# Post-norm of a sublayer's outputs: inverse root formed per token as a column and spread by TensorE, with one weight cast moved ahead of it on ScalarE

## The chip, the cores and the metric

The kernel runs on one NeuronCore of a Trainium2 chip. The metric is the device time of one execution in microseconds (us), as the median of several executions. Lower is better.

## The reference, cut to what matters

Two layers, each of three sublayers: a feed-forward block, a mixer of two head groups, a second feed-forward block. Each sublayer has an RMS norm before it and one behind it:

```python
def rms_norm(x, g=None):
    y = xf * lax.rsqrt(jnp.mean(jnp.square(xf), axis=-1, keepdims=True) + EPS)
...
def gated_post(x, o, g, mods, j, coef):
    return x + coef * mods[:, 3 * j + 2, None] * rms_norm(o, g)
...
    h = modulated_pre(x, norm_pre[l, 0], mods, 0)
    x = gated_post(x, swiglu(h, ffn_w1[l, 0], ffn_w3[l, 0], ffn_w2[l, 0]), norm_post[l, 0], mods, 0, 0.5)
```

There are 512 prompt frames and 32 sample frames, so 544 tokens in all, and D_MODEL is 1024. The change concerns `rms_norm(o, g)` inside `gated_post`: one number for each token, 1/sqrt(mean of squares + eps), by which all 1024 outputs of that token are multiplied. It happens six times in the program.

## The kernel before, in words

Activations lie transposed: features on the 128 partitions, tokens along the free dimension, so `x` is 8 tiles of 128 x 544. Sums over features are therefore sums over partitions, and TensorE makes them with a matmul.

Weights come from memory in chunks, into the two slots of `raw`. ACT (ScalarE) casts a chunk to `w_hi` (`high`, L936 to L947), POOL (GpSimd) forms the rest `w_lo` (`low`, L446), and PE (TensorE) multiplies with both. SP (SyncE) issues the load of a chunk when the low part of the chunk two before it is made (L343 to L344). Every engine has its own hand-written instruction stream; semaphores join them, and within a stream the order is that of the code.

The outputs of a sublayer come as 8 tiles (`out_tiles` on PE and on ACT), alternating between PSUM banks 0 and 1 and banks 2 and 3. For each, ACT squares the tile into `wide_s` (L1026) and evicts it to `o_buf` (`o_ffn` or `o_mix`), scaled by the gate (L1030, L1032). POOL adds the squares of tiles 0 to 6 into `squares` (L453, L457).

After the last output tile comes what is called the turn-over here:

- PE sums over partitions with a full matrix of ones, first `squares` (L633), then the last tile's squares (L635), both through `add_squares` (L543). Banks 4 and 5 then hold, on every one of the 128 partitions, the same 544 sums.
- ACT takes the square root of all 128 x 544 (`root_of`, L950).
- DVE (VectorE) takes the reciprocal of 128 x 544 (L1290) into banks 4 and 5, and then, for each of 8 tiles, forms the product with it (L1297). It adds the even tiles and the last to `x` (L1301), POOL the other odd ones (`add_odd`, L472).
- ACT starts the next sublayer with `pre_scale`: two small casts (L958), the cast of the next sublayer's second chunk (L960; the first was cast during the last output tile), then `h_hi` from each tile of `x` as it comes (L965), and squares of `x` (L975).
- POOL makes `w_lo` of the next sublayer's first two chunks (L477) ahead of its own additions to `x`.
- PE starts with `first_tiles` (L556 to L566) when `h_hi` of tile 0 and the two chunks are ready. DVE makes `h_lo` (L1316).

After the last sublayer there is no next one, and `x` is written out.

## Time and profile before

| | |
|---|---|
| median of 3 executions | 2578.21 us |
| lowest and highest | 2574.72 and 2578.86 us |
| the profiled execution, its own time | 2575.32 us |
| its span, first to last instruction | 2573.5 us |
| PE busy | 2374.8 us (92%) |
| DVE, POOL, ACT busy | 1318.2, 893.4, 812.6 us |
| granted TensorE clock, mean | 0.977 of full |

The profiled execution is one execution, and its time is that of the device, some 1.8 us above its span. A busy share is an average over the whole program; what sets the end is read from the chain of work that ended last, and at a given place from the idle time in front of an instruction and the name of what ended it.

### The profile page before, as it was taken

How to read it: one execution, taken by the hardware profiler on the slowest of the kernel's cores; microseconds unless marked ns; L12 is line 12 of the kernel's file. 1: busy time of each engine (PE TensorE's matmuls, PEld its weight loads, DVE VectorE, ACT ScalarE, POOL GpSimd, SP SyncE). 2: the span in 40 equal slices, each digit the busy share in tenths (PEclk: the TensorE clock that was granted, in tenths of full speed). 3: DMA queues.
4: the chain of work that ended last, by engine and by line, in shares of the span. 5: the costliest groups of instructions: out<-in, count | busy, mean ns of one | idle time of the engine just before them, and what ended most of it. 6: DMA issues, size and time to landing. Idle time of an engine off the chain costs nothing.

```text
span 2573.5 us, 43848 instructions
## 1 busy us (share of the span) xinstructions
PE 2374.8 (92%) x17486; PEld 2231.6 (87%) x17486; DVE 1318.2 (51%) x2006; ACT 812.6 (32%) x1371; POOL 893.4 (35%) x384
## 2 busy tenths in 40 slices
PE   1999999899788899999989999989988898999996
PEld 1999999899456899999989999989964588999996
DVE  7333379784473333337253335986835515333552
ACT  2322322433223433223243223234323334223321
POOL 1333334443000544344444343444420034333342
PEclk9999999999899999999999999999989999999998
DMA  6222268323100122226312224761220011222551
GB/s 222 76 88 84 90 236 280 116 88 112 33 1 6 61 89 83 89 89 248 122 57 82 90 81 155 281 221 66 82 71 33 1 50 59 89 84 87 182 197 57
DMA packets 71507, 272.48 MB, mean 106 GB/s; under 512 B 8640, under 2 KB 10048, under 8 KB 70528
## 3 DMA queue, kind: packets, MB, share of 16 engines
q1 hardware_dynamic: 71424, 271.35, 30.6%
q8 instruction: 55, 0.90, 0.1%
q14 instruction: 28, 0.23, 0.0%
HBM read 267.87 MB, written 3.45 MB: 105 GB/s over the span
## 4 chain that ended last, share of the span: by engine, by line
PE 75%; DVE 12%; issue 6%; ACT 3%; DMA 1%; POOL 1%; DVEq 0%; SPq 0%; POOLq 0%; ACTq 0%
PE ps L534 21%; PE ps L533 21%; PE ps L537 21%; PE ps L543 2%; PE ps L831 2%; PE ps L875 2%; DVE ret_q L1407 1%; PE ps L827 1%; DVE ret_k L1407 1%; DVE wide_v L1297 1%; DVE x L1301 1%; PE ps L566 1%; DVE wide_v L1256 1%; POOL w_lo L446 1%; DVE ps L1290 1%
## 5 line engine op out<-in xcount | busy, mean ns | idle before, releaser
L446 POOL TENSOR_TENSOR w_lo<-raw,w_hi 128x1024 fp32r<-128x1024 f32 (+1 forms) x304 | 790.7, 2601 | 1609.8 <-ACT w_hi L947 1294.1
L533 PE MATMUL ps<-h_hi,w_hi 128*128 128x274 f32 x3296 | 897.0, 290 | 5.3 <-DVE z_tmp L1376 5.3
L534 PE MATMUL ps<-h_lo,w_hi 128*128 128x274 f32 x3296 | 900.7, 290 | 0.0
L537 PE MATMUL ps<-h_hi,w_lo 128*128 128x274 f32 x3296 | 686.7, 289 | 0.0
L533 PEld LDWEIGHTS ps<-h_hi,w_hi 128*128 128x128 f32 x3296 | 624.9, 190 | 6.8 <-issue 6.7
L534 PEld LDWEIGHTS ps<-h_lo,w_hi 128*128 128x128 f32 x3296 | 621.7, 189 | 0.2
L947 ACT CAST w_hi<-raw 128x1024 fp32r<-128x1024 f32 (+1 forms) x236 | 268.7, 1138 | 877.3 <-PE ps L537 689.8
L537 PEld LDWEIGHTS ps<-h_hi,w_lo 128*128 128x128 f32 x3296 | 522.0, 188 | 0.0
L533 PE MATMUL ps<-u_hi,w_hi 128*128 128x272 f32 x1408 | 382.4, 289 | 12.9 <-POOL w_lo L446 12.9
L534 PE MATMUL ps<-u_lo,w_hi 128*128 128x272 f32 x1408 | 380.8, 289 | 0.0
L1256 DVE CUSTOM_DVE_ANT_0 wide_v<-ada_w,ps 128x1024 bf16<-128x1024 f32 x288 | 332.1, 1217 | 46.5 <-DMA ada_w<-in_ada 29.3
L1334 DVE TENSOR_TENSOR wide_v<-ps,wide_rinv 128x548 f32<-128x548 f32 x88 | 64.1, 729 | 449.3 <-PE ps L537 449.3
L537 PE MATMUL ps<-u_hi,w_lo 128*128 128x272 f32 x1408 | 292.5, 289 | 0.0
L533 PEld LDWEIGHTS ps<-u_hi,w_hi 128*128 128x128 f32 x1408 | 266.0, 189 | 14.6 <-POOL w_lo L446 14.5
L534 PEld LDWEIGHTS ps<-u_lo,w_hi 128*128 128x128 f32 x1408 | 265.6, 189 | 0.0
L1339 DVE SCALAR_TENSOR_TENSOR wide_v<-wide_v,wide_s 128x512 f32<-128x512 f32 (+1 forms) x176 | 194.2, 1142 | 110.2 <-ACT wide_s L998 110.2
L537 PEld LDWEIGHTS ps<-u_hi,w_lo 128*128 128x128 f32 x1408 | 220.5, 188 | 0.0
L556 PE MATMUL ps<-h_hi,w_hi 128*128 128x274 f32 x192 | 63.0, 350 | 91.7 <-ACT h_hi L965 69.9
L1290 DVE RECIPROCAL ps<-root 128x544 f32<-128x544 f32 x6 | 21.4, 3560 | 217.6 <-ACT root L950 217.6
L556 PEld LDWEIGHTS ps<-h_hi,w_hi 128*128 128x128 f32 x192 | 44.3, 231 | 98.2 <-issue 74.1
L1001 ACT CAST u_hi<-wide_v 128x544 f32 (+1 forms) x88 | 57.0, 648 | 214.1 <-DVE wide_v L1339 214.1
L940 ACT CAST w_hi<-raw 128x1024 fp32r<-128x1024 f32 x68 | 71.1, 1046 | 167.1 <-PE ps L537 102.1
(219 smaller groups left out, 2552.5 us busy)
## 6 DMA issues: line engine op xcount, KB each, us to landing
raw<-in_w_up SPq DMA_DIRECT2D x176, 512.0 KB, 3.3
ada_w<-in_ada SPq DMA_DIRECT2D x160, 512.0 KB, 4.4
raw<-in_w_dn SPq DMA_DIRECT2D x64, 704.0 KB, 4.7
raw<-in_w_mix SPq DMA_DIRECT2D x64, 512.0 KB, 3.3
decay<-in_decay SPq DMA_DIRECT2D x2, 2048.0 KB, 8.3
x<-in_x SPq DMA_DIRECT2D x1, 2176.0 KB, 9.1
rope_tab<-in_rope SPq DMA_DIRECT2D x2, 1088.0 KB, 4.9
out_y<-x SPq DMA_DIRECT2D x1, 2176.0 KB, 7.3
```

The costliest lines, as they stand in the source:

```text
L446: pool.tensor_tensor(w_lo[:, slot, 0:width], raw[:, slot, 0:width], w_hi[:, slot, 0:width].bitcast(F32), ALU.subtract).then_inc(lo_done.se ...
L533: pe.matmul(ps[:, bank + t, 0:half], wh, hi[:, n], start=start, stop=False)
L534: pe.matmul(ps[:, bank + t, 0:half], wh, lo[:, n], start=False, stop=False)
L537: last = pe.matmul(ps[:, bank + t, 0:half], wl, hi[:, n], start=False, stop=stop)
L543: last = pe.matmul(ps[:, bank + t, 0:HT], mat[:, :], src[:, t * HT:(t + 1) * HT], start=start, stop=stop)
L556: pe.matmul(ps[:, 2 * w + t, 0:HW], w_hi[:, w, k * P:(k + 1) * P], h_hi[:, k, n], start=k == 0, stop=False)
L940: nc.scalar.copy(w_hi[:, slot, 0:width], raw[:, slot, 0:width]).then_inc(hi_done.sem, 1)
L947: nc.scalar.copy(w_hi[:, k, 0:width], raw[:, k, 0:width]).then_inc(hi_done.sem, 1)
L1001: nc.scalar.copy(u_hi[:, bass.ds(i * 2 + f, 1), :].rearrange("p a n -> p (a n)"), tmp_v[:, f, :]).then_inc(up_hi.sem, 1)
L1256: v_.tensor_tensor_reduce(junk[v], ada_w[:, t, :], c_row, 1.0, 0.0, ALU.mult, ALU.add, acc[:, v, t:t + 1]).then_inc(ada_done.sem, 1)
L1334: v_.tensor_tensor(halves(wide_v[:, f, :]), wide_pair(4 * f + 2), halves(wide_rinv[:, :]), ALU.mult)\
L1339: v_.scalar_tensor_tensor(out=wide_v[:, f, at], in0=wide_v[:, f, at], scalar=wide_v[:, f, T + 2 * v:T + 2 * v + 1], in1=wide_s[:, f, at], ...
```

## The change

- PE: the sums are formed with the tokens on the partitions. For each of five blocks of 128 tokens (at 0, 128, 256, 384 and 416, the last one overlapping) the squares are the stationary operand and one column of ones is the moving one (`token_sums`). The result is 128 x 5 in a corner of bank 5.
- ACT: the root is of 128 x 5 (`token_root`). It stands between the last square and the last tile's evictions, no longer behind them.
- ACT: the cast of the next sublayer's second chunk stands between the last square and `token_root`, no longer in `pre_scale` (except for the first sublayer, which has nothing ahead of it).
- DVE: the reciprocal is of 128 x 5.
- PE: five transposes (`spread`) of those columns, each broadcast along the free dimension, put the 544 inverses on all 128 partitions of banks 4 and 5, now as 544 neighbouring columns.
- DVE: each product waits for its own tile's eviction, no longer for all eight ahead of the first.

```diff
+TOK_AT = [0, P, 2 * P, 3 * P, T - P]
+TOK = len(TOK_AT)
+SUM_AT = 2 * NS
...
+            def token_sums(src, bank, start, stop):
+
+                for b, at in enumerate(TOK_AT):
+                    last = pe.matmul(by_token(bank)[:, b:b + 1], src[:, at:at + P], ones[:, 0:1],
+                                     start=start and b == 0, stop=stop, skip_group_check=True)
+                return last
+
+            def spread(l, n, bank):
+
+                pe.wait_ge(inverted.sem, inverted.at(l, 2 * n + 2))
+                for b in range(4):
+                    pe.transpose(ps[:, bank, b * P:(b + 1) * P], tok_inv[:, b:b + 1].to_broadcast([P, P]), ident[:, :])
+                pe.transpose(ps[:, bank + 1, 0:NS], tok_inv[P - NS:P, 4:5].to_broadcast([NS, P]),
+                             ident[P - NS:P, P - NS:P]).then_inc(inv_spread.sem, 1)
...
-                add_squares(squares[:, :], 4, True, False, ones)
+                token_sums(squares[:, :], 4, True, False)
                 pe.wait_ge(out_sq.sem, out_sq.at(l, (j + 1) * KD))
-                add_squares(tmp_s[:, 1, :], 4, False, True, ones).then_inc(sums.sem, 1)
+                token_sums(tmp_s[:, 1, :], 4, False, True).then_inc(sums.sem, 1)
+                spread(l, j, 4)
...
+            def token_root(l, n, bank):
+                nc.scalar.activation(tok_root[:, :], by_token(bank), ACT.Sqrt, bias=eps[:, 0:1], scale=1.0 / D)\
+                    .then_inc(rooted.sem, 1)
...
-                high(l, next_chunk + 1, 1, KD * P)
+                if not (l or j):
+                    high(l, next_chunk + 1, 1, KD * P)
...
                     nc.scalar.activation(halves(tmp_s[:, mm, :]), pair(2 * mm), ACT.Square).then_inc(out_sq.sem, 1)
+                    if m == KD - 1:
+                        if next_chunk is not None:
+                            high(next_chunk[0], next_chunk[1] + 1, 1, KD * P)
+                        act.wait_ge(sums.sem, sums.at(l, (j + 1) * SUMS))
+                        token_root(l, 2 * j + 1, 4)
...
-                act.wait_ge(sums.sem, sums.at(l, (j + 1) * SUMS))
-                root_of(l, rooted, 2 * j + 1, 4, D)
...
-                    v_.reciprocal(out_inv, halves(root[:, :])).then_inc(inverted.sem, 1)
-                    dve.wait_ge(inverted.sem, inverted.at(l, 2 * j + 2))
-                    dve.wait_ge(out_ev.sem, out_ev.at(l, (j + 1) * KD))
+                    v_.reciprocal(tok_inv[:, :], tok_root[:, :]).then_inc(inverted.sem, 1)
+                    dve.wait_ge(inv_spread.sem, inv_spread.at(l, j + 1))
                     for m in range(KD):
+                        dve.wait_ge(out_ev.sem, out_ev.at(l, j * KD + m + 1))
...
-                        v_.tensor_tensor(halves(tmp_v[:, m % 2, :]), halves(o_buf[:, m, :]), out_inv, ALU.mult)\
+                        v_.tensor_tensor(tmp_v[:, m % 2, :], o_buf[:, m, :], along(4), ALU.mult)\
```

On ACT, at the last output tile of the first feed-forward block and the start of the mixer, these instructions stand in the stream before the change (`L940` casts a weight chunk, `L1026` squares, `L1030` and `L1032` evict, `L950` is the root, `L965` makes `h_hi`):

```order
L940 CAST w_hi<-raw 128x1024
L1026 ACTIVATE wide_s<-ps 128x544
L1030 ACTIVATE o_ffn<-ps,mul_post 128x272
L1030 ACTIVATE o_ffn<-ps,mul_post 128x240
L1032 ACTIVATE o_ffn<-ps,mul_post 128x32
L950 ACTIVATE root<-ps,eps 128x544
L958 CAST h_hi<-mods 128x8x2 x2
L940 CAST w_hi<-raw 128x1024
L965 ACTIVATE h_hi<-x,mul_pre 128x512
```

The same stretch of ACT's stream with the change (the line numbers are those of the changed kernel; `L968` casts, `L1059` squares, `L982` is `token_root`, `L998` makes `h_hi`):

```order
L968 CAST w_hi<-raw 128x1024
L1059 ACTIVATE wide_s<-ps 128x544
L968 CAST w_hi<-raw 128x1024
L982 ACTIVATE tok_root<-ps,eps 128x5
L1068 ACTIVATE o_ffn<-ps,mul_post 128x272
L1068 ACTIVATE o_ffn<-ps,mul_post 128x240
L1070 ACTIVATE o_ffn<-ps,mul_post 128x32
L990 CAST h_hi<-mods 128x8x2 x2
L998 ACTIVATE h_hi<-x,mul_pre 128x512
```

The second cast moved from behind the root to directly behind the square, and the root moved ahead of the three evictions.

On PE, between the last output tile and `first_tiles` of the mixer, this stands in the stream before (one row of this listing is a matmul of the program, which the trace shows as two passes where its operands are plain 32-bit floats):

```order
L537 MATMUL ps<-u_hi,w_lo 128x272 x2
L626 REGISTER_ALU
L626 COMPARE_AND_BRANCH
L543 MATMUL ps<-squares,ones 128x272 x2
L543 MATMUL ps<-wide_s,ones 128x272 x2
L556 MATMUL ps<-h_hi,w_hi 128x274
```

And this with the change:

```order
L549 MATMUL ps<-u_hi,w_lo 128x272 x2
L653 REGISTER_ALU
L653 COMPARE_AND_BRANCH
L562 MATMUL ps<-ones,squares 128x1 x5
L562 MATMUL ps<-ones,wide_s 128x1 x5
L570 MATMUL ps<-ident,tok_inv 128x128 x4
L571 MATMUL ps<-ident,tok_inv 128x32
L583 MATMUL ps<-h_hi,w_hi 128x274
```

Four wide matmuls became ten of one column, and five transposes, which wait for DVE, follow them ahead of the next sublayer's first matmul.

## Rows read from the trace of the kernel before

**Rows 1.** The page: the chain that ended last, shares of the span by engine.
```profile
PE 75%; DVE 12%; issue 6%; ACT 3%; DMA 1%; POOL 1%; DVEq 0%; SPq 0%; POOLq 0%; ACTq 0%
```

**Rows 2.** Instructions by line: the reciprocal (L1290) and the roots (L950); ns min/median/max.
```profile
L1290 DVE RECIPROCAL ps<-root x6: 3560/3560/3561, 473.8 to 2551.4; 128x544 f32<-128x544 f32 x6
...
L950 ACT ACTIVATE root<-ps,eps x16: 694/716/717, 73.1 to 2550.7; 128x544 f32<-128x544 f32 x16
```

**Rows 3.** Timeline of ACT, first turn-over: start us, us, what, [idle before <-releaser].
```profile
471.19 0.62 ACT L1026 ACTIVATE wide_s<-ps 128x544 f32<-128x544 f32 x1 [5.77 <-PE ps L537]
471.71 0.83 ACT L1030 ACTIVATE o_ffn<-ps,mul_post 128x272 f32<-128x272 f32 x2
...
473.09 0.72 ACT L950 ACTIVATE root<-ps,eps 128x544 f32<-128x544 f32 x1 [0.36 <-PE ps L543]
...
473.90 1.04 ACT L940 CAST w_hi<-raw 128x1024 fp32r<-128x1024 f32 x1
478.95 0.72 ACT L965 ACTIVATE h_hi<-x,mul_pre 128x512 fp32r<-128x512 f32 x1 [4.00 <-DVE x L1301]
```

**Rows 4.** Timeline of DVE, the same turn-over.
```profile
477.43 0.72 DVE L1297 TENSOR_TENSOR wide_v<-o_ffn,ps 128x544 f32<-128x544 f32 x1
478.19 0.72 DVE L1301 TENSOR_TENSOR x<-x,wide_v 128x544 f32<-128x544 f32 x1
478.83 1.34 DVE L1297 TENSOR_TENSOR wide_v<-o_ffn,ps 128x544 f32<-128x544 f32 x2
480.21 1.34 DVE L1301 TENSOR_TENSOR x<-x,wide_v 128x544 f32<-128x544 f32 x1
```

**Rows 5.** Timeline of POOL, the same turn-over.
```profile
475.02 2.34 POOL L446 TENSOR_TENSOR w_lo<-raw,w_hi 128x1024 fp32r<-128x1024 f32 x1 [7.13 <-ACT w_hi L940]
479.62 1.34 POOL L472 TENSOR_TENSOR x<-x,wide_v 128x544 f32<-128x544 f32 x1 [2.26 <-DVE wide_v L1297]
```

**Rows 6.** Timeline of PE and of its weight loads (PEld), the same turn-over.
```profile
470.99 1.08 PE L543 MATMUL ps<-squares,ones 128*128 128x272 f32 x4
471.90 1.14 PE L543 MATMUL ps<-wide_s,ones 128*128 128x272 f32 x4
...
471.86 0.76 PEld L543 LDWEIGHTS ps<-wide_s,ones 128*128 128x128 f32 x4 [0.23 <-ACT wide_s L1026]
```

**Rows 7.** Timelines of PE and PEld in the mixer: transposes, three weight loads, small matmuls.
```profile
640.97 1.91 PE L699 MATMUL ps<-ident,ret_v 128*128 128x128 f32 x16
...
708.25 0.30 PEld L831 LDWEIGHTS ps<-wide_s,q_pe 128*128 128x128 f32 x2
708.46 0.26 PEld L827 LDWEIGHTS ps<-kv,q_abs 128*128 128x128 f32 x1
...
652.17 0.42 PE L730 MATMUL ps<-ret_ss,v_tok 32*64 32x32 f32 x2
652.52 0.42 PE L731 MATMUL ps<-q_cross,state_in 128*64 128x32 f32 x2
```

**Rows 8.** Instructions by line, ns min/median/max: a small eviction, small reciprocal, the products.
```profile
L1032 ACT ACTIVATE o_ffn<-ps,mul_post x32: 288/296/299, 361.1 to 2550.0; 128x32 f32<-128x32 f32 x32
...
L1543 DVE RECIPROCAL inv_sum<-exp_sum x68: 152/153/165, 711.8 to 2066.8; 128x1 f32<-128x1 f32 x68
...
L1297 DVE TENSOR_TENSOR wide_v<-o_ffn,ps x32: 705/709/721, 477.4 to 2564.3; 128x544 f32<-128x544 f32 x32
```

**Rows 9.** Windows (busy PE PEld DVE ACT POOL, clock, DMA share, GB/s), first, last of four; SP timeline.
```profile
466.00:471.10 5.10, 5.10 (x43) 5.10 (x42) 2.37 (x10) 0.00 (x0) 1.89 (x1) 1.00 0.00 0
...
2123.00:2127.10 4.10, 4.10 (x34) 4.10 (x33) 0.00 (x0) 0.56 (x1) 2.56 (x2) 1.00 0.00 0
...
1283.72 18.47 SPq L344 DMA_DIRECT2D raw<-in_w_up  x3
```

**Rows 10.** Windows of PE alone (length, busy, granted clock, DMA share, GB/s), first turn-over.
```profile
473.10:479.90 6.80, 0.00 (x0) 0.74 0.81 303
479.90:483.00 3.10, 3.07 (x12) 0.50 0.08 30
```

More of the change, by code:

```diff
@@ L161, in streaming_trunk @@
         eps_root = sb("eps_root", [P, 1])
+        tok_root = sb("tok_root", [P, TOK])
+        tok_inv = sb("tok_inv", [P, TOK])
         neg_row = sb("neg_row", [P, 64])
@@ L223, in halves, with by_token, along @@
             return t.rearrange("p (t n) -> p t n", t=2)
-        out_inv = pair(4)
+        def by_token(bank):
+            return ps[:, bank + 1, SUM_AT:SUM_AT + TOK]
+        def along(bank):
+            return ps[:, bank:bank + 2, :].rearrange("p b n -> p (b n)")[:, 0:T]
         def c_psum(v):
@@ L249, in streaming_trunk @@
         inverted = signal("inverted", 6)
+        inv_spread = signal("inv_spread", 3)
         h_high = signal("h_high", 54)
```

## The prediction

> **What bounds the kernel now.** I read the page first. The chain that ended last lies on PE for 75% and on DVE for 12% [rows 1]. So PE's own matmuls are most of the time, and a change that touches none of the large ones can only win where PE stands still. The list of instructions by line says where that is for this change: the reciprocal of the outputs' norm runs six times, 3.56 us each [rows 2]. Six is five turn-overs between sublayers and the end.
>
> The timelines of one turn-over give the order of events. PE's last product allows ACT to square at 471.19 [rows 3]. PE adds the summed squares at 470.99 and the last tile's from 471.86 on, ending at 471.90 + 1.14 = 473.04 [rows 6]. The root starts at 473.09, idle before it because of PE, and lasts 0.72 [rows 3]. The reciprocal runs from 473.84 to 477.40, and the first product starts at 477.43 [rows 2, 4]. `x` of tile 0 is done at 478.19 + 0.72 = 478.91, and ACT, idle for 4.00 us, starts `h_hi` at 478.95 on it [rows 3, 4]. Nothing that is not on this list is waited for: POOL's `w_lo` of the second chunk is ready at 475.02 + 2.34 = 477.36 [rows 5], well ahead of `h_hi`. So the chain through the turn-over is square, sums, root, reciprocal, product, and from square to first product it takes 477.43 - 471.19 = 6.24 us. The other turn-overs have the same pieces within some 0.05 us.
>
> **The change part by part**, on the clock of this turn-over.
>
> *The sums.* What was four passes of 272 columns for each operand becomes ten passes of one column (a matmul of plain floats is two passes: the listing's x2 is the trace's x4 [rows 6]). With one column each pass should last no longer than its weight load. Where nothing else holds them, the first of three loads of 128 columns starts at 708.25 and the third at 708.46, so they follow each other by 0.105 [rows 7]. I take 0.108: the sixteen transposes, which load 128 columns each, follow at (1.91 - 0.27)/15 = 0.109 too [rows 7], where 0.27 is the length of one. The first ten passes start at 470.99 and the tenth at 470.99 + 9 x 0.108 = 471.96. The square is there at 471.86, so the second ten are now slightly held by the first: their first starts at 472.07, the tenth at 473.04. Of the old last pass (0.39 us for 272 columns spaced 0.23) 0.16 was not columns, so the sums are there at 473.20, 0.16 later than before. This part loses.
>
> *The moved cast.* It takes ACT from 471.71 to 472.75 (1.04 us [rows 3]), and the root can't start before 473.24 anyway, so it is hidden with 0.5 us to spare. It takes nothing else's place: the evictions that stood there are wanted only by products that come later. What could spoil it is its chunk not having landed, since `token_root` now stands behind it in ACT's queue. In four of the five turn-overs (windows of 4.0 to 5.1 us that end at the square, all with a DMA share of 0.00) the DMA engines move nothing before the square, so the chunk had landed by then [rows 9]. In the remaining one it was the first of three issued from 1283.72 on [rows 9], and the square comes at 1295.5, twelve us later. Its other wait, that PE has used the slot, is the one that the square has.
>
> *The root.* An eviction of 128 x 32 takes 0.296 us [rows 8], and the root of 544 columns 0.716, so a column costs (0.716 - 0.296)/512 = 0.0008 and 5 columns about 0.27. From 473.24 to 473.51, where it was 473.09 to 473.81.
>
> *The reciprocal.* 0.153 us for one column [rows 8] and 3.560 for 544 [rows 2]: 0.0063 a column, 0.18 for five. From 473.54 to 473.72 instead of to 477.40. This is the part that pays: 3.38 us.
>
> *The spread.* New on the path. DVE to PE takes 0.05 (ACT's square ends at 471.81, PE loads at 471.86 [rows 3, 6]), the first load 0.11, then four transposes 0.109 apart, the last lasting 0.27, and the short fifth ends at about the same time: 473.77 + 0.11 + 0.33 + 0.30 = 474.51. With 0.04 to DVE the first product starts at 474.55.
>
> *The page's word against it.* The Trainium skill (TensorE: Matmul & The Clock Gate, Part 4: PE-mode transpose) gives about 390 ns for an isolated 128 x 128 transpose and says that transposes do not hold the clock up. By that, five would take 1.95 us instead of 0.74, each turn-over would gain 1.7 us instead of 2.9, and the time would be near 2568. The trace here shows 16 in 1.91 us, directly behind other matmuls.
>
> *The waits.* Each product now waits for its own eviction. The last one ends at about 473.4 + 1.0 = 474.5, long before the eighth product, so the extra semaphores cost nothing; if they did, it would be some hundredths of a us each.
>
> So a turn-over gains 477.43 - 474.55 = 2.88 us. Is it kept? `x` of tile 0 comes 2.88 earlier, at 476.03. POOL's low part moves with the cast to about 472.83 until 475.17, so POOL is free for its own additions, as it was, and PE has both chunks. ACT waits 4.00 us for `x` now and would wait about 1.1. What follows, `h_hi`, `h_lo`, squares and PE's stream, hangs on `x` and moves as a whole. The weight loads behind it move earlier or stay, and there is slack: the third chunk is in flight during the reciprocal, and is not used until after `first_tiles`. The end of the program has no cast, but the same chain, so it gains the same: the output is issued when the last `x` is there.
>
> Six times 2.88 is 17.3 us. The profiled execution had 2575.32 us, so the sum gives 2558.0 in its terms. It lies 2.9 under the median of the three runs shown, 2578.21, which with the same gain is 2560.9. I predict **2561 us**.
>
> **Bounds of the unknown costs.** PE's one-column passes and the spread are not in the trace. At best the sums end before the cast does and the root starts at 472.70, 0.54 earlier; but then DVE's first addition meets POOL. An addition that meets a running POOL addition takes 1.34 us, one alone 0.72 [rows 4, 5], while the products take 0.705 to 0.721 in all cases [rows 8]. POOL is busy until 475.17, so the first addition can't be done before about 475.9, which caps the gain at 3.0; only at the end, where no cast and no low part runs, is it 3.4. That is 18.4 us together. At worst passes follow each other as the small matmuls of the mixer do, two in 0.35 us [rows 7], 0.175 each: sums at 474.5, with the root at 0.30 and the spread at 1.2 the first product at 476.5, 0.93 us gained, 5.6 together.
>
> *The second rule.* The Trainium skill (SBUF — State Buffer, Who interferes with whom) says that a DVE instruction with two SBUF inputs contends with a GpSimd one that reads SBUF, and one with a single SBUF input does not. The trace agrees: 0.72 against 1.34 for additions, no difference for products. By that rule the low part may lie beside the first product but not beside the first addition. It ends 0.14 us ahead of it, so nothing is added.
>
> **The rivals.**
>
> 1. *PE's new steps cost more than their weight loads*, because one-column passes or transposes after a pause are not spaced like a full stream. For it: no row shows either in this place, and the small matmuls are at 0.175. Against it: these switch between 32- and 128-row operands, and a run of equal ones does not. It gives 0.9 to 2.2 us each: 2565 to 2573. Chance 0.14.
>
> 2. *The product is slowed by POOL's low part*, which now runs beside it and no longer beside the reciprocal. If the first product took 1.34 like an addition, 0.62 is lost in five turn-overs: 2564. Against it: all 32 of the feed-forward products lie within 0.016 us of each other [rows 8], though the second of a pair runs beside POOL's addition (the pair from 478.83 to 480.17, POOL from 479.62 [rows 4, 5]). Chance 0.06.
>
> 3. *The gain is given back in `first_tiles`*. PE idles 6.8 us, its granted clock averages 0.74 there and is 0.50, the lower level, until 483 [rows 10]. If the lower clock began at the same time and lasted longer against the work, or something that does not hang on `x` set the pace, little would be left: 2575 to 2578. Against it: twelve matmuls at the lower clock took 3.07 us [rows 10], so the eight of a tile at most 2.05, and `x` of tile 1 comes at 479.62 + 1.34 = 480.96 [rows 5], 2.05 behind tile 0's: PE keeps pace even then, and its pause gets shorter. Chance 0.05.
>
> 4. *Slower: ACT's queue is blocked by the moved cast.* If the chunk landed late, root, reciprocal, spread and evictions would all wait behind it. There are 0.5 us of cover and then the 2.88 of gain, so it turns against the change where the chunk lands more than 3.9 us after the square starts, at 475.1 here; at 480, five turn-overs would lose 5 us each and the time would be 2601. Against it: in every turn-over it had landed at least 4 us before the square. Chance 0.03.
>
> **How the numbers follow.** The main case has 0.72, with its own range of 2557 to 2565: the cap of 18.4 us from the lower runs, and half a us of error in each gain. The range for 8 in 10 reaches from 2555 into rival 1, to 2570. A difference under 0.2%, 5.2 us, can't be told from no change on this kernel. The main case and rivals 1 and 2 are faster by more than that, 0.92; rival 3 is the 0.05 of no change; rival 4 is the 0.03 of slower.
>
> **What the profile of the changed kernel would show.** The reciprocal at about 0.18 us, six times, and the first product 3.3 to 3.5 us after the last square's start, where it was 6.24. Ten passes 0.11 apart for each operand; a root at about 0.27 whose idle time PE ends, not the cast; five transposes in about 0.75 us. ACT's idle time before `h_hi` down from 4.00 to about 1.1, and the same distance as now from `x` of tile 0 to PE's `h_lo` matmuls. The moved cast follows the square without a wait for a DMA. I would be wrong if passes of one column are spaced 0.17 or more, if the root waits for the cast's chunk, or if the distance from the first product to PE's steady stream grows by what the turn-over gained.

## The result, and the profile after

| | before | changed |
|---|---|---|
| median | 2576.51 us, 4 executions | 2562.71 us, 4 executions |
| lowest and highest | 2574.72 and 2578.86 us | 2559.62 and 2563.99 us |
| profiled execution, its own time and its span | 2575.32 and 2573.5 us | 2563.67 and 2561.9 us |

The ratio is 0.9945, with a 95% interval of 0.9933 to 0.9957. That is 14.2 us gained (11 to 17) by the ratio, 13.8 by the medians; forecast were 17.3 us of gain and a time of 2561.

The page of the changed kernel first: the shares of the chain that ended last, by engine.

```profile
span 2561.9 us, 44088 instructions
...
PE 77%; DVE 11%; issue 6%; ACT 2%; DMA 1%; POOL 1%; DVEq 0%; SPq 0%; POOLq 0%; ACTq 0%
```

Then its instructions by line and shape (count, ns min/median/max, first and last start): what took the place of [rows 2], and the spread.

```profile
L1326 DVE RECIPROCAL tok_inv<-tok_root x6: 190/190/191, 475.4 to 2542.3; 128x5 f32<-128x5 f32 x6
...
L982 ACT ACTIVATE tok_root<-ps,eps x6: 266/267/267, 475.1 to 2542.0; 128x5 f32<-128x5 f32 x6
...
L570 PE MATMUL ps<-ident,tok_inv x24: 272/273/474, 475.6 to 2542.9; 128*128 128x128 f32 x24
```

Against [rows 1] the chain has two points more on PE, one less on DVE and one less on ACT, as six reciprocals of 3.56 us became six of 0.19 and the path is shorter. The third line has a spread that the other two lack: the four transposes of one place take 421 to 474 ns, the others 272 to 323.

Timelines of the turn-over ahead of the second feed-forward block (start us, us, what; in brackets the idle time before and what ended it). The same events one turn-over earlier in the kernel before are [rows 3] to [rows 6]. ACT:

```profile
874.31 0.62 ACT L1059 ACTIVATE wide_s<-ps 128x544 f32<-128x544 f32 x1 [3.54 <-PE ps L549]
874.83 1.04 ACT L968 CAST w_hi<-raw 128x1024 fp32r<-128x1024 f32 x1
876.43 0.27 ACT L982 ACTIVATE tok_root<-ps,eps 128x5 f32<-128x5 f32 x1 [0.57 <-PE ps L562]
...
879.34 0.93 ACT L998 ACTIVATE h_hi<-x,mul_pre 128x512 fp32r<-128x512 f32 x2 [1.54 <-DVE x L1337]
```

PE:

```profile
874.11 1.17 PE L562 MATMUL ps<-ones,squares 128*128 128x1 f32 x10
875.14 1.25 PE L562 MATMUL ps<-ones,wide_s 128*128 128x1 f32 x10
876.97 0.65 PE L570 MATMUL ps<-ident,tok_inv 128*128 128x128 f32 x4 [0.58 <-DVE tok_inv L1326]
877.55 0.24 PE L571 MATMUL ps<-ident,tok_inv 32*128 32x32 f32 x1
```

DVE:

```profile
877.83 0.72 DVE L1333 TENSOR_TENSOR wide_v<-o_mix,ps 128x544 f32<-128x544 f32 x1 [0.91 <-PE ps L571]
878.58 0.72 DVE L1337 TENSOR_TENSOR x<-x,wide_v 128x544 f32<-128x544 f32 x1
```

POOL:

```profile
875.94 2.35 POOL L458 TENSOR_TENSOR w_lo<-raw,w_hi 128x1024 fp32r<-128x1024 f32 x1 [2.71 <-ACT w_hi L968]
```

From square to first product there are now 877.83 - 874.31 = 3.52 us, where there were 6.24. The cast follows the square without a wait, and the root waits for PE, not for the cast. The first product lies beside POOL's low part (875.94 to 878.29) and still takes 0.72; the first addition starts 0.29 us behind its end and takes 0.72 as well. `h_hi` comes 5.03 us behind the square, where it was 478.95 - 471.19 = 7.76 [rows 3]. So the 2.72 us reach `h_hi` undiminished, and they are still whole further on: the reciprocal of the next pre-norm starts 26.9 us behind the square where it was 29.6, in every turn-over but the fourth (27.5).

Square to first product, in us, in all six places of a profiled execution, worked out from the starts of the two:

| | 1 | 2 | 3 | 4 | 5 | end |
|---|---|---|---|---|---|---|
| before | 6.24 | 6.24 | 6.24 | 6.24 | 6.24 | 6.24 |
| changed | 3.53 | 3.52 | 3.52 | 4.06 | 3.52 | 3.52 |

The fourth place is 0.54 us longer. Windows of PE around it (length, busy, granted clock, DMA share, GB/s) say why: between the sums and the transposes the granted clock falls to 0.50, the lower of TensorE's two levels, 1.2 GHz, and the five transposes run at it. PE had been busy without a gap until the sums' end, at 1721.97, and the clock is at full until 1722.46, so that the fall comes in PE's pause for root and reciprocal.

```profile
1715.00:1720.00 5.00, 5.00 (x43) 1.00 0.00 0
1720.00:1722.50 2.50, 1.97 (x18) 0.99 0.70 181
1722.50:1724.00 1.50, 1.36 (x5) 0.50 0.98 413
```

The turn-overs of this execution gained 5 x 2.72 + 2.18 = 15.8 us, but its span only 2573.5 - 2561.9 = 11.6. Some 4 us were lost where the change has no instruction. The steady streams, which have the same matmuls in both kernels, show a part of it. Windows (length, busy, granted clock, DMA share, GB/s) in an up and in a down projection of the kernel before:

```profile
920.00:1140.00 220.00, 220.00 (x1729) 1.00 0.26 86
2460.00:2540.00 80.00, 80.00 (x639) 1.00 0.36 126
```

and of the changed one:

```profile
920.00:1140.00 220.00, 220.00 (x1722) 1.00 0.25 85
2460.00:2540.00 80.00, 80.00 (x642) 1.00 0.30 103
```

PE is busy throughout at the full clock in both, and in the up projection it does seven matmuls fewer in 220 us. From start to start they stand 127.92 ns apart, where it was 127.36. In the down projections it is the other way round, 125.3 for 125.8. With some 8100 matmuls in the steady part of the up projections and 4224 in the down projections of the feed-forward blocks that makes about 4.5 - 2.1 = 2.4 of the 4 us (an estimate from these counts). The prediction knew nothing of this.

### The profile page after: what moved, and what is told of

Read it like the earlier page. It is cut to its first block, busy times and chain, and to the rows that moved or that the text cites. A ratio compares the mean times of both kernels' runs of the same rounds, so it can differ in the third digit from the quotient of the medians.

```text
span 2561.9 us, 44088 instructions
## 1 busy us (share of the span) xinstructions
PE 2387.9 (93%) x17588; PEld 2247.4 (88%) x17588; DVE 1295.2 (51%) x2006; ACT 809.5 (32%) x1371; POOL 892.4 (35%) x384
## 4 chain that ended last, share of the span: by engine, by line
PE 77%; DVE 11%; issue 6%; ACT 2%; DMA 1%; POOL 1%; DVEq 0%; SPq 0%; POOLq 0%; ACTq 0%
PE ps L545 22%; PE ps L549 22%; PE ps L546 21%; PE ps L859 2%; PE ps L903 2%; PE ps L555 1%; DVE ret_q L1443 1%; PE ps L855 1%; DVE ret_k L1443 1%; PE ps L593 1%; DVE wide_v L1333 1%; DVE wide_v L1292 1%; PE ps L769 1%; DVE x L1337 1%; DVE h_lo L1352 1%
## 5 line engine op out<-in xcount | busy, mean ns | idle before, releaser
L968 ACT CAST w_hi<-raw 128x1024 fp32r<-128x1024 f32 x68 | 71.1, 1046 | 170.7 <-PE ps L549 113.6
```

The source lines that it names most:

```text
L968: nc.scalar.copy(w_hi[:, slot, 0:width], raw[:, slot, 0:width]).then_inc(hi_done.sem, 1)
```

## The experiments

Three theories for the 4 us: **A**, the pace belongs to the execution and varies from one to the next; **B**, it comes from the changed turn-overs; **C**, it comes from where the large operands lie in SBUF, since the two new tiles `tok_root` and `tok_inv` (20 bytes a partition each, 64 together as placed) stand ahead of the tiles of `h` and `u` and push them up by 64 bytes. The others concern the terms of the turn-over. Times in brackets are of the kernel before on the same chip, 17 or 23 executions each.

**The kernel before, once more** (no edit).

> The kernel before, once more, for its trace. In the two traces at hand the passes of the up stages follow each other by 127.36 ns before and by 127.91 ns with the change, in every stage and already in the first, which lies ahead of anything that the change touches; over the whole program that is 3 to 4 us. Theory A (the pace belongs to the execution, not to the program): this execution can show either pace, and its time goes with it, near 2575 with 127.4 or near 2578.5 with 127.9; from the last square's start to the first product it is 6.24 us in all six places either way. Theory B (the changed program slows PE's stream): the pace is 127.4 here.

2577.46 us (2577.1), ratio 1.0001 (0.9992 to 1.0010). Its window of PE:

```profile
920.00:1140.00 220.00, 220.00 (x1730) 1.00 0.26 86
```

The pace is 127.36 ns again.

**The changed kernel, once more** (no edit).

> The changed kernel, once more, with more rounds. Theory A: either pace; where it is 127.4 the time is near 2560, where it is 127.9 near 2563.5; square to first product 3.52 us, or 4.06 where the granted clock falls before the transposes; the ratio to the kernel before over more runs comes out at 0.994 or a little under (a gain of 15 to 16 us). Theory B: the pace is 127.9 in this trace too, and the gain stays at 12 to 14 us.

2562.49 us, ratio 0.9943 (0.9930 to 0.9957). Its window of PE:

```profile
920.00:1140.00 220.00, 220.00 (x1722) 1.00 0.26 84
```

127.92 ns again. A falls: the pace goes with the program. The clock does not: here five of the six places are longer, by 0.4 to 0.6 us (3.93, 3.96, 4.06, 4.07, 3.53, 4.11). The timeline of the fourth shows where, the four transposes taking 1.11 us instead of 0.65:

```profile
1722.85 1.11 PE L570 MATMUL ps<-ident,tok_inv 128*128 128x128 f32 x4 [0.59 <-DVE tok_inv L1326]
```

**The norm alone**, the cast left where it was.

```diff
-                if not (l or j):
-                    high(l, next_chunk + 1, 1, KD * P)
+                high(l, next_chunk + 1, 1, KD * P)
...
                     if m == KD - 1:
-                        if next_chunk is not None:
-                            high(next_chunk[0], next_chunk[1] + 1, 1, KD * P)
                         act.wait_ge(sums.sem, sums.at(l, (j + 1) * SUMS))
                         token_root(l, 2 * j + 1, 4)
```

> The norm by token as in the changed kernel, but the cast of the second next chunk stays in pre_scale, behind the evictions. The theory that the cast's place matters through POOL and DVE's additions: the first product still comes 3.5 us after the square, but the cast only runs at 3.4 to 4.4 us, POOL's low part at 4.5 to 7.3, so POOL's first addition to x comes at about 7.3 instead of 5.7 after the square, DVE's second addition waits for POOL, and PE's first matmuls of the second chunk wait for the low part. Of 2.73 us in each of five turn-overs 1.0 to 1.6 are lost, the end keeps its 2.7: the whole gain is 8 to 11 us, 5 to 8 less than the changed kernel. The rival, that the low part is hidden wherever it stands: same time as the changed kernel, within 1 us.

2570.57 us (2577.1), ratio 0.9977 (0.9966 to 0.9989). The square is at 874.82 and the first product 3.53 us later, so the shorter norm is there in full. What follows it is not. POOL in this kernel:

```profile
879.34 2.71 POOL L458 TENSOR_TENSOR w_lo<-raw,w_hi 128x1024 fp32r<-128x1024 f32 x1 [5.58 <-ACT w_hi L968]
882.01 1.81 POOL L484 TENSOR_TENSOR x<-x,wide_v 128x544 f32<-128x544 f32 x1
```

and ACT:

```profile
878.19 1.07 ACT L968 CAST w_hi<-raw 128x1024 fp32r<-128x1024 f32 x1
879.86 0.93 ACT L997 ACTIVATE h_hi<-x,mul_pre 128x512 fp32r<-128x512 f32 x2 [0.60 <-DVE x L1334]
883.86 1.76 ACT L997 ACTIVATE h_hi<-x,mul_pre 128x512 fp32r<-128x512 f32 x4 [3.07 <-POOL x L484]
```

The cast comes at 878.19, so POOL's low part ends at 882.05, and its addition of tile 1 stands behind it and ends 1.81 us later, at 883.82. ACT idles 3.07 us for it. The next pre-norm's reciprocal comes 28.49 us behind the square instead of 26.91: 1.58 us lost, in five turn-overs 7.9. The move of the cast is worth that, half of the gain.

**The cast alone**, with the wide root and the wide reciprocal. The wide root moves too, ahead of the last tile's evictions, as in the changed kernel.

```diff
-                high(l, next_chunk + 1, 1, KD * P)
+                if not (l or j):
+                    high(l, next_chunk + 1, 1, KD * P)
...
+                    if m == KD - 1:
+                        if next_chunk is not None:
+                            high(next_chunk[0], next_chunk[1] + 1, 1, KD * P)
+                        act.wait_ge(sums.sem, sums.at(l, (j + 1) * SUMS))
+                        root_of(l, rooted, 2 * j + 1, 4, D)
...
-                act.wait_ge(sums.sem, sums.at(l, (j + 1) * SUMS))
-                root_of(l, rooted, 2 * j + 1, 4, D)
```

> The kernel before with only the cast moved ahead of the wide root, and the root ahead of the last evictions, the norm's arithmetic unchanged. The theory that the path is square, sums, root, reciprocal: the root still starts 1.90 us after the square (the cast ends at 1.56), the first product still comes at 6.24, and the time is that of the kernel before within 1 us. The rival, that part of the changed kernel's gain is the earlier cast and low part itself: 2 us or more faster than before.

2575.21 us (2577.1), ratio 0.9994 (0.9985 to 1.0003), and 6.24 us in all six places. ACT:

```profile
873.77 1.04 ACT L940 CAST w_hi<-raw 128x1024 fp32r<-128x1024 f32 x1
875.15 0.72 ACT L950 ACTIVATE root<-ps,eps 128x544 f32<-128x544 f32 x1 [0.34 <-PE ps L543]
```

The cast is hidden behind the sums with 0.34 us to spare, and alone brings nothing that can be measured: the reciprocal had covered the low part. Apart, the norm is worth 6 us (with `h` and `u` 64 bytes further, as in the changed kernel) and the cast nothing that can be told from zero; together they are worth 14.

**The place alone**: the kernel before, with an unused tile of 64 bytes a partition where the new tiles stood.

```diff
         eps_root = sb("eps_root", [P, 1])
+        unused = sb("unused", [P, 16])
         neg_row = sb("neg_row", [P, 64])
```

> The kernel before with nothing changed but an unused tile of 64 bytes per partition, put where the changed kernel has its two small tiles, so that h_hi, h_lo, u_hi, u_lo begin 64 bytes later, as there. The traces so far showed that the passes of the up stages follow each other by 127.36 ns in every execution with the old norm and by 127.92 ns in every one with the norm by token, ahead of the first turn-over too, and those of the down stages by 125.8 and 125.3 ns. Theory C (the place of the operands in SBUF sets it): 127.92 and 125.3 here, each up stage 1.1 us longer (279.7 instead of 278.6 us), the down stages 0.6 shorter, in all 2 to 3 us slower than before, the turn-overs as before (6.24). Theory D (it is PE's code, its length or order): 127.36 and 125.8, time as before.

2578.37 us (2576.09), ratio 1.0008 (0.9998 to 1.0017). PE's window:

```profile
920.00:1140.00 220.00, 220.00 (x1723) 1.00 0.26 86
```

127.92 and 125.3 ns, the changed kernel's pace, with no instruction of its own. B falls and C holds for the pace. The ratio alone would not have told it: its interval contains 1.

**The new tiles between those of `h` and of `u`**: `h` lies where it did before, `u` 64 bytes further.

```diff
-        tok_root = sb("tok_root", [P, TOK])
-        tok_inv = sb("tok_inv", [P, TOK])
...
         sb("h_space", [P, size // 4])
+        tok_root = sb("tok_root", [P, TOK])
+        tok_inv = sb("tok_inv", [P, TOK])
```

> The changed kernel with its two small tiles allocated between the h tiles and the u tiles: h_hi and h_lo begin where they did before, u_hi and u_lo 64 bytes later, and the instructions are the same. Theory C: 127.36 ns in the up stages and 125.3 ns in the down stages, the better one of each; each up stage 1.1 us shorter than in the changed kernel, 4 to 5 us in all, so 2558, ratio to before 0.9925. Theory D: 127.92 ns and the time of the changed kernel.

2556.76 us (2576.09), ratio 0.9935 (0.9922 to 0.9949). PE's window:

```profile
920.00:1140.00 220.00, 220.00 (x1729) 1.00 0.26 86
```

Up projections at 127.36 ns again, down projections at 125.3: each follows the place of its own operand. The weights lie ahead of all of these tiles and stayed where they were. The median is 6 us below the changed kernel's, the ratio only 0.1%, where 0.2% was expected, and the two intervals overlap; here too it is the pace that tells.

**Sums of 64 equal columns** instead of one, of which `token_root` reads each 64th (that line and the width of the sums' tile are not shown).

```diff
+COLS = 64
...
-                    last = pe.matmul(by_token(bank)[:, b:b + 1], src[:, at:at + P], ones[:, 0:1],
+                    last = pe.matmul(by_token(bank)[:, COLS * b:COLS * (b + 1)], src[:, at:at + P], ones[:, 0:COLS],
```

> The changed kernel, but each of the token sums' passes moves 64 columns of ones instead of one (the results beside the first are not used). In the traces of the changed kernel the granted clock fell just ahead of the transposes in one of six places and in five of six, and those have 3.93 to 4.1 us from the square to the first product instead of 3.52. If it falls because TensorE does so little in the one-column passes ahead of it: with 64 columns, which lie behind the weight loads (0.112 us apart still), the clock stays up until the transposes are done, all six places show 3.50 to 3.55, and 0.5 to 2.5 us are won. The rival, that the pause for root and reciprocal alone brings it down: as many places near 4.0 as before, same time.

2562.89 us (2576.09), ratio 0.9958 (0.9946 to 0.9970). All six places are at 3.58 us, and no transpose takes over 323 ns (by line):

```profile
L571 PE MATMUL ps<-ident,tok_inv x24: 272/273/323, 474.3 to 2538.8; 128*128 128x128 f32 x24
```

So the profiled execution did what was hoped, at 0.05 us more for each place. The median did not: the forecast gain over the changed kernel isn't seen, and the two intervals overlap.

**One pass for each block of tokens**: the last sum of squares and the last tile's squares are written as float32r, a rounded form that PE takes in one pass (five matmuls in the trace for five blocks, where there were ten), into the space of `root` and `wide_rinv`, and two columns of ones are moved. These columns, `ones_r`, are a new small tile too, and put `h` and `u` 96 bytes beyond a multiple of 128. The squares are thus rounded in this kernel.

```diff
+        rm, size = overlay([[("root", [P, T], F32), ("wide_rinv", [P, TW], F32)],
+                            [("last_sq", [P, T], F32R), ("sum_sq", [P, T], F32R)]])
...
-                token_sums(squares[:, :], 4, True, False)
+                token_sums(sum_sq[:, :], 4, True, False)
...
-                token_sums(tmp_s[:, 1, :], 4, False, True).then_inc(sums.sem, 1)
+                token_sums(last_sq[:, :], 4, False, True).then_inc(sums.sem, 1)
```

> The changed kernel, but the two operands of the token sums (the sum of squares of tiles 0 to 6, and the last tile's squares) are written as float32r, into the space of root and wide_rinv, and move two columns: one pass each, five for each operand instead of ten. If the ten passes at 0.112 us are what stands between the square and the root: the first five end before the square does, the second five take 0.56 instead of 1.12 us, the wait behind the first ones (0.18) is gone, and the root could start at 1.4 us after the square instead of 2.13, but then the moved cast (until 1.56) is what it waits for. Root at 1.56, first product at 2.95. The first addition then meets POOL's low part (until 4.0 after the square) and is done at 4.6 instead of 5.0: of 0.57 us only 0.4 are kept in five places, 0.55 at the end, 2.5 us in all less than the changed kernel. If POOL's low part does not hold the addition: 3.4 us.

2551.21 us (2576.09), ratio 0.9909 (0.9896 to 0.9923). DVE in this kernel, with the square at 869.59:

```profile
872.45 0.72 DVE L1339 TENSOR_TENSOR wide_v<-o_mix,ps 128x544 f32<-128x544 f32 x1 [0.91 <-PE ps L574]
873.21 0.94 DVE L1343 TENSOR_TENSOR x<-x,wide_v 128x544 f32<-128x544 f32 x1
```

and POOL:

```profile
871.22 2.35 POOL L461 TENSOR_TENSOR w_lo<-raw,w_hi 128x1024 fp32r<-128x1024 f32 x1 [2.71 <-ACT w_hi L972]
```

Square to product is 2.86 us in four of the five turn-overs (3.40 in the first) and 2.83 at the end. The effect from which the prediction worked out its cap is there: POOL is busy until 873.57, the addition begins 0.36 us ahead of that and takes 0.94 instead of 0.72. Of 0.67 us saved 0.45 arrive at `h_hi`. The cap itself was a little low: it let the whole 0.72 of the addition follow POOL's end, while here it ends 0.58 behind it, and `h_hi` comes 7.76 - 4.60 = 3.16 us earlier than in the kernel before, where the cap was 3.0. The time is 11 us below the changed kernel's, where the expectation had 2.5 less; most of the rest is the place of `h` and `u`, as the table below shows.

**The root behind the last evictions**, the cast first.

```diff
                         if next_chunk is not None:
                             high(next_chunk[0], next_chunk[1] + 1, 1, KD * P)
-                        act.wait_ge(sums.sem, sums.at(l, (j + 1) * SUMS))
-                        token_root(l, 2 * j + 1, 4)
...
+                act.wait_ge(sums.sem, sums.at(l, (j + 1) * SUMS))
+                token_root(l, 2 * j + 1, 4)
```

> The changed kernel with token_root put back behind the last tile's evictions; the cast stays directly behind the square. In five turn-overs the evictions now run from 1.52 to 2.53 us after the square and the root can't start before 2.53, where it started at 2.13: first product at 3.93 instead of 3.52, 0.4 us lost each. At the end there is no cast, the evictions are done by 1.5, nothing is lost. In all 2.0 us slower than the changed kernel, near 2564.5, where the granted clock stays up. The rival, that the root's place beside the evictions is worth nothing: first product at 3.52.

2563.44 us (2574.84), ratio 0.9948 (0.9932 to 0.9965). 3.77 us where the clock stays (4.31 in the fourth place), 3.53 at the end, where no cast stands. The place of the root is worth 0.24 us in a turn-over, where 0.4 was expected:

```profile
876.66 0.28 ACT L982 ACTIVATE tok_root<-ps,eps 128x5 f32<-128x5 f32 x1
```

ACT's instructions overlap at their ends, so that behind cast and evictions the root starts at 876.66, with the square at 874.31 as in the changed kernel, where the root had started at 876.43. The median can't tell it.

**Ten more passes on the path**: `squares` summed once more, behind the last square.

```diff
                 pe.wait_ge(out_sq.sem, out_sq.at(l, (j + 1) * KD))
+                token_sums(squares[:, :], 4, True, False)
                 token_sums(tmp_s[:, 1, :], 4, False, True).then_inc(sums.sem, 1)
```

> The changed kernel with the ten one-column passes over the sum of squares made once more, after the wait for the last square, so that ten more passes stand on the path. If a pass costs the spacing that the trace shows, 0.1117 us, the root starts 1.12 us later and the first product comes at 4.64 us after the square (5.2 where the granted clock falls before the transposes, which the longer stretch of small passes should make commoner): 6.7 to 9.5 us slower than the changed kernel in all. If the passes were hidden by the cast, which ends at 1.56: no change.

2570.51 us (2574.84), ratio 0.9985 (0.9975 to 0.9995). PE:

```profile
872.34 2.29 PE L562 MATMUL ps<-ones,squares 128*128 128x1 f32 x20
874.49 1.46 PE L562 MATMUL ps<-ones,wide_s 128*128 128x1 f32 x10
876.53 1.11 PE L570 MATMUL ps<-ident,tok_inv 128*128 128x128 f32 x4 [0.58 <-DVE tok_inv L1327]
```

By the medians it is 8 us slower than the changed kernel, 10 by the ratios; 6.7 to 9.5 was expected. In three places square to product is 4.64 to 4.67, 1.12 us more for ten passes. In the other three (5.08 to 5.39) the clock falls, as in the rows shown: the last ten passes take 1.46 for 1.25, the transposes 1.11 for 0.65.

**One pass, 64 columns, and `h` and `u` 96 bytes beyond a multiple of 128** (0 for both in the kernel before, 64 for both in the changed one). Against the one-pass kernel:

```diff
+COLS = 64
...
-        ones_r = sb("ones_r", [P, 2], F32R)
+        ones_r = sb("ones_r", [P, COLS + 8], F32R)
```

> The best version that the runs point to: one float32r pass per block (as in e8_one_pass), each moving 64 columns of ones (as in e7_wide_ones), and h and u tiles beginning 96 bytes past a multiple of 128, where e8_one_pass had them. First product at 2.86 to 2.92 us after the square in all six places, none at 3.4; passes of the up stages 127.2 ns apart, of the down stages 125.0. Time that of e8_one_pass or up to 0.5 us less, 2550.5; ratio to before 0.990.

2551.45 us (2574.84), ratio 0.9908 (0.9894 to 0.9922). 2.86 us in all six places. In the second of them the clock falls right behind the last transpose:

```profile
872.97 0.24 PE L575 MATMUL ps<-ident,tok_inv 32*128 32x32 f32 x1
```

It is at full until 873.31, and a window of PE from there has it at the lower level:

```profile
873.40:875.00 1.60, 0.00 (x0) 0.50 0.00 0
```

The square was at 870.38. Its time is that of the one-pass kernel, which already had both tiles at 96.

**The changed kernel with `h` and `u` at 96**, by an unused tile of 32 bytes.

```diff
         tok_inv = sb("tok_inv", [P, TOK])
+        unused = sb("unused", [P, 8])
```

> The changed kernel with an unused tile of 32 bytes, so that the h and u tiles begin 96 bytes past a multiple of 128 (before: 0; the changed kernel: 64). e8_one_pass had this place and 127.22 ns between the passes of the up stages and 125.0 in the down stages, but also other instructions on PE. If the place alone sets it: the same 127.2 and 125.0 here, up stages of 278.3 us instead of 279.7, 6 to 7 us less than the changed kernel in all, 2556. If it was the instructions: 127.9 and 125.3 and the changed kernel's time.

2554.70 us (2574.84), ratio 0.9918 (0.9903 to 0.9933): 32 unused bytes make the changed kernel 8 us shorter by the medians, 0.27% or 7 us by the ratios. PE's window:

```profile
920.00:1140.00 220.00, 220.00 (x1732) 1.00 0.26 86
```

What the place does, over all profiled executions. The pace is from start to start of neighbouring large matmuls; the last column adds the four stretches that hold the feed-forward blocks, each from the first product of the norm before it (for the first stretch, from the program's start) to its last output tile's square, so that no turn-over is in it:

| place of `h`, `u` beyond a multiple of 128 bytes | up, ns | down, ns | four stretches, us |
|---|---|---|---|
| 0, 0: before, again, cast alone | 127.36 | 125.8 | 1723.6, 1727.0, 1722.8 |
| 64, 64: changed, again, place alone, 64 columns, root last, more passes | 127.92 | 125.3 | 1727.6, 1728.9, 1728.2, 1725.8, 1727.1, 1727.1 |
| 0, 64: tiles between | 127.36 | 125.3 | 1721.7 |
| 96, 96: one pass, with 64 columns, place 96 | 127.22 | 125.0 | 1721.3, 1720.9, 1721.2 |

The means are 1724.5, 1727.5, 1721.7 and 1721.1. The paces repeat from execution to execution, the stretches less so: the first two rows overlap in part (1722.8 to 1727.0 and 1725.8 to 1728.9). (The norm alone, also at 64, is left out of the row: its lost 1.58 us lie inside these stretches.)

## Why the prediction was right, and where it was off

**The reciprocal**: right. 0.18 us forecast, 0.19 measured. The root, 0.27, is 0.267.

**The cast**: right. It follows the square without waiting for a DMA (rival 4 is out), and the root, idle before it for PE, doesn't wait for the cast. Left out of the argument was how much the move is worth: without it 1.58 us of each 2.72 are lost again to POOL's queue.

**The sums**: right in kind, a little small. The prediction took 0.108 us a pass; ten more passes cost 1.12, so 0.112. The root starts 876.43 - 874.31 = 2.12 us behind the square, where 2.05 was forecast.

**The spread**: 0.83 us forecast from the reciprocal's end to the product, 0.91 measured. The forecast had the short fifth transpose end together with the fourth; it ends at 877.79, 0.17 us behind it. Together these two terms make a turn-over worth 2.72 and not 2.88: 16.3 us and not 17.3. Rival 1, passes at 0.175 us, is out; the second to the fourth transpose of this place stand 0.109 us apart, as the sixteen of [rows 7], while the clock is full. The 390 ns that the Trainium skill (TensorE: Matmul & The Clock Gate, Part 4: PE-mode transpose) gives for an isolated transpose are for bf16, and as a price for each of several fp32 ones they don't hold: four take 0.65 us here, and 1.11 at the lower clock. The prediction left out that the same section gives about 275 ns for a transpose within a kernel; the trace agrees, with 272 to 273 for most.

**The product beside POOL's low part** (rival 2): not slowed, 0.72. The one-pass kernel shows both halves of the rule of the Trainium skill (SBUF — State Buffer, Who interferes with whom), from which the prediction had its cap: the addition, with two SBUF inputs, takes 0.94 where it overlaps POOL, the product 0.72 throughout.

**"The gain is given back in `first_tiles`"** (rival 3): no. `h_hi` and the next norm's reciprocal come 2.72 us earlier, like the product. ACT's idle time before `h_hi` was 1.54, not about 1.1. The forecast had only taken the gain off the 4.00; but what ACT does from the root's start to that wait has become shorter too, 879.34 - 1.54 - 876.43 = 1.37 us for 478.95 - 4.00 - 473.09 = 1.86 [rows 3], by a smaller root and by evictions in place of the cast, and the root starts 0.22 us later behind the square.

**What failed** are two assumptions that stood in no term. One: "that the same gain" in six places is the whole sum, with nothing changed elsewhere. It left out that two new small tiles move the large ones. The place of `h` and `u` cost 3.0 us over the four feed-forward stretches of the profiled executions (1727.5 for 1724.5, means of few executions that scatter by 3 to 4 us), and about 2.4 by the paces alone. Two: that the spread runs at the full clock. In 36 places with one-column double passes (the changed kernel twice, the norm alone, tiles between, root last, place 96) the granted clock fell ahead of or in the transposes in 11, at up to 0.6 us each; in the changed kernel that is 0.5 us in one profiled execution and 2.5 in the other.

The account of the 14.2 us: 16.3 in the turn-overs at the full clock, less 0.5 to 2.5 for the clock, less 3.0 for the place, is 10.8 to 12.8, at the lower end of what was measured (11 to 17). The 1.4 to 3.4 us between that and 14.2 are within the interval and have no cause shown. The predicted time was met to 1.7 us although the gain was 3 us too large, because the base it was taken from, 2578.21, lies 1.7 us above the median of the four executions that the ratio compares. That it was met so closely is luck.

Open stays why the place in SBUF changes the pace, and why the 64 columns, which kept every place at 3.58 us in their profiled execution, brought nothing in the median. With one column 11 of 36 places lost clock ahead of or in the transposes, and with 64 none of 12, but that doesn't show that the columns are the cause. The executions differ much among themselves (none of six, and five of six, with the same passes). And in the one-pass kernel with 64 columns the clock fell 2.93 us behind the square in the second place, as in the rows shown there. Its transposes were through by 2.83; with double passes they lie at 2.66 to 3.49, and falls at 2.85 and 3.03 cost 0.4 and 0.2 us in two of the 11 places. So that kernel kept at least this place because it was done sooner, not because the clock stayed.

The one-pass kernels are the fastest, 2551.2 and 2551.5 us: 11 us below the changed kernel. The changed kernel with the same place, 2554.7, lies between: 8 us come from the place and 3.5 from the passes by these medians, 7 and 2.5 by the ratios.

## What to carry to other kernels

Where one number per row or token is needed, form it as a column, do the costly elementwise operation on that, and spread it with TensorE afterwards: a reciprocal of 544 columns cost 3.56 us on the path and five columns 0.19, with 0.9 for the spread. When a step gets shorter, look for what it had covered: here a cast and POOL's low part had lain beside it, and half of the gain hung on moving them. And a new small tile moves all that are allocated behind it: hold the places of the matmuls' operands fixed when two kernels are compared, and try them as a parameter of their own.

## What was not expected of the hardware

The place of a matmul's operands in SBUF sets the spacing of a steady stream at the full clock with PE busy all the time: 127.36, 127.92 and 127.22 ns for moving tiles of 274 columns at 0, 64 and 96 bytes beyond a multiple of 128, and 125.8, 125.3 and 125.0 for those of 272. The two kinds don't rank the places alike.

The granted clock falls in every turn-over: with the wide norm 4.2 to 6.9 us behind the square (24 places in four profiled executions), with the changed norm and one-column double passes 1.9 to 5.3 (36 places). There the five transposes can meet it, at 2.66 to 3.49. The windows around the fourth turn-over in the second execution of the changed kernel (length, busy, clock, DMA share, GB/s), busy in full and at 1.00 until the sums' end at 1722.26, then with the fall 0.3 us into PE's pause:

```profile
1718.00:1722.20 4.20, 4.20 (x38) 1.00 0.25 48
1722.20:1724.30 2.10, 1.42 (x6) 0.58 0.99 419
```

The pause isn't needed for it. In the first place of the changed kernel with `h` and `u` at 96 the clock falls while PE, without a gap before, is still in the one-column passes, which end at 474.05:

```profile
470.00:473.80 3.80, 3.80 (x36) 1.00 0.27 39
473.85:474.05 0.20, 0.20 (x2) 0.50 0.80 305
```
